# Where the split weights of a hybrid decoder layer begin in SBUF: 48 bytes past a multiple of 64 in place of 0

## What is computed

```python
h = rmsnorm(x, norm1_g)
z = h @ w_in                        # 2048 -> 16400 columns: u, c, b, q, k, v, o, gates, g_a, g_b
a_out = b * causal_conv(c * u)      # 3 taps, with a state of 2 rows for the samples
b_out = sigmoid(o) * mlstm(q, k, v, gates)   # 8 heads, key width 128, value width 256
x = x + (sigmoid(g_a) * a_out + sigmoid(g_b) * b_out) @ w_out      # 2048 x 2048
h2 = rmsnorm(x, norm2_g)
up = causal_conv(h2 @ w_up, state_ffnconv)   # 2048 -> 2 * 5632 columns, 3 taps
x = x + (silu(up[..., 5632:]) * up[..., :5632]) @ w_down           # 5632 x 2048
y = rmsnorm(x, norm_f_g)
```

## Time and profile before

| | us |
|---|---|
| median of 3 runs | 1697.74 |
| profiled execution, its device time | 1698.14 |
| its span, from the first to the last instruction | 1696.4 |
| TensorE matmuls busy | 1684.1 (99%), 13712 matmuls |
| VectorE busy | 1194.5 (70%) |
| ScalarE busy | 767.4 (45%) |
| GpSimd busy | 477.6 (28%) |
| mean granted TensorE clock | 0.998 of 2.4 GHz |

### The profile page before, as it was taken

One profiled execution on the slowest core, in us unless ns is written; L12 is line 12 of the kernel. 1 busy time (PEld: TensorE's weight loads), 2 busy tenths in 40 slices (PEclk: granted clock), 3 DMA queues, 4 the chain that ended last, 5 costly groups with the idle time before them and its releaser, 6 DMA issues.

```text
span 1696.4 us, 37171 instructions
## 1 busy us (share of the span) xinstructions
PE 1684.1 (99%) x13712; PEld 1677.6 (99%) x13712; DVE 1194.5 (70%) x1901; ACT 767.4 (45%) x916; POOL 477.6 (28%) x501
## 2 busy tenths in 40 slices
PE   9999999999999999999999999999999999999997
PEld 8999999999999999999999999999999999999997
DVE  5875857677585766758688877777555777777554
ACT  6545435353443535344445554544333334334443
POOL 4422415242241524224333222222000222222220
PEclk9999999999999999999999999999999999999999
DMA  8788786868878687877766666666666666566663
GB/s 208 189 223 199 199 212 172 212 176 219 192 190 217 166 216 180 212 192 193 195 180 181 190 178 183 180 180 174 183 183 181 180 179 183 174 184 175 186 178 121
DMA packets 591309, 318.80 MB, mean 188 GB/s; under 512 B 17756, under 2 KB 586060, under 8 KB 589156
## 3 DMA queue, kind: packets, MB, share of 16 engines
q1 hardware_dynamic: 578564, 292.99, 64.0%
q10 hardware_dynamic: 10592, 21.57, 5.1%
q0 software_dynamic: 2064, 2.92, 0.8%
HBM read 305.09 MB, written 12.78 MB: 187 GB/s over the span
## 4 chain that ended last, share of the span: by engine, by line
PE 99%; DMA 0%; ACT 0%; DVE 0%; SPq 0%; issue 0%; ACTq 0%; DVEq 0%
PE strip L1526 32%; PE strip L1530 32%; PE strip L1534 32%; PE aux L1408 1%; PE strip L1457 0%; DMA w_raw<-in_w_in 0%; PE aux L1587 0%; PE aux L1477 0%; PE strip L1470 0%; PE aux L1617 0%; PE aux L1616 0%; PE aux L1630 0%; PE aux L1621 0%; PE aux L1614 0%; PE aux L1622 0%; PE aux L1613 0%
## 5 line engine op out<-in xcount | busy, mean ns | idle before, releaser
L714 ACT ACTIVATE w_hi<-w_raw 128x1024 fp32r<-128x1024 f32 x557 | 588.7, 1060 | 786.1 <-PE strip L1534 753.1
L987 DVE TENSOR_TENSOR w_lo<-w_raw,w_hi 128x1024 fp32r<-128x1024 f32 x556 | 710.3, 1282 | 295.0 <-ACT w_hi L714 292.6
L1526 PE MATMUL strip<-xh,w_hi 128*128 128x268 f32 (+1 forms) x2016 | 291.0, 286 | 0.0
L1530 PE MATMUL strip<-xl,w_hi 128*128 128x268 f32 (+1 forms) x2016 | 290.0, 286 | 0.0
L1534 PE MATMUL strip<-xh,w_lo 128*128 128x268 f32 (+1 forms) x2016 | 290.0, 286 | 0.0
L1526 PEld LDWEIGHTS strip<-xh,w_hi 128*128 128x128 f32 x2016 | 265.1, 188 | 0.2
L1530 PEld LDWEIGHTS strip<-xl,w_hi 128*128 128x128 f32 x2016 | 265.2, 188 | 0.0
L1534 PEld LDWEIGHTS strip<-xh,w_lo 128*128 128x128 f32 x2016 | 265.2, 188 | 0.0
L1526 PE MATMUL strip<-x2h,w_hi 128*128 128x266 f32 x1408 | 200.2, 284 | 0.0
L1530 PE MATMUL strip<-x2l,w_hi 128*128 128x266 f32 x1408 | 199.9, 284 | 0.0
L1534 PE MATMUL strip<-x2h,w_lo 128*128 128x266 f32 x1408 | 199.9, 284 | 0.0
(11 more groups left out here) (330 smaller groups left out, 1525.5 us busy)
## 6 DMA issues: line engine op xcount, KB each, us to landing
w_raw<-in_w_in SPq DMA_DIRECT2D x256, 512.0 KB, 4.5
w_raw<-in_w_up SPq DMA_DIRECT2D x176, 512.0 KB, 4.1
w_raw<-in_w_down SPq DMA_DIRECT2D x64, 512.0 KB, 4.1
w_raw<-in_w_out SPq DMA_DIRECT2D x32, 512.0 KB, 4.7
w_raw<-in_w_down SPq DMA_DIRECT2D x32, 384.0 KB, 3.4
out<-c_st ACTq DMA_DIRECT2D x8, 1024.0 KB, 7.1
c_st<-in_state_mlstm_C ACTq DMA_DIRECT2D x7, 1024.0 KB, 10.8
rb<-scratch_rows ACTq DMA_DIRECT2D x8, 270.0 KB, 5.1
```

What stands on the lines that cost most here:

```text
L714: act.activation(w_hi[:, slot, :], w_raw[:, slot, :], ACT.Copy).then_inc(hi_done, 1)
L987: v.tensor_tensor(w_lo[:, slot, :], w_raw[:, slot, :], w_hi[:, slot, :].bitcast(f32), ALU.subtract).then_inc(lo_done, 1)
L1526: pe.matmul(bank[b][:, 0:c1 - c0], w_hi[:, slot, w], rh[:, k0 + k, c0:c1], start=(first and k == 0), stop=False)
L1530: pe.matmul(bank[b][:, 0:c1 - c0], w_hi[:, slot, w], rl[:, k0 + k, c0:c1], start=False, stop=False)
```

## The change

`w_hi` and `w_lo` each get a room of 16896 bytes (512 more than before), begin 32 bytes into it, have slots of 4160 bytes (`WW = 1040` words, 65 x 64 bytes), and leave out the first 4 words of a slot (`WO`). A weight tile so begins at 48 modulo 64 in place of 0. Slots that lay a multiple of 256 bytes apart now lie 4160 bytes apart, which is 64 more than such a multiple. `w_raw` and its DMAs stay as they are. Numbers, kinds, shapes and waits of all instructions are the same; only the addresses change.

`pre_f` is no longer persistent: it lies in the region where the attention has `v_1`, `p_main` and `p_rest`. With 1024 bytes more for the weights and 2816 less for `pre_f` the tensors between them move (`ident`, `ones`, `vecs` by 1024, those after `pre_s` by -1792), and the region by -2048 bytes, which keeps its place modulo 512.

```diff
+    WO = 4
+    WW = KU * P + 16
...
-        w_hi = sb("w_hi", [P, RING, KU * P], f32r)
-        w_lo = sb("w_lo", [P, RING, KU * P], f32r)
+        w_hi_room = (nc.sbuf_base + 31) // 32 * 32
+        sb("w_hi_room", [P, RING * KU * P + P])
+        w_hi = nc.alloc_sbuf_tensor_at("w_hi", [P, RING, WW], f32r, offset=w_hi_room + 32)
+        w_lo_room = (nc.sbuf_base + 31) // 32 * 32
+        sb("w_lo_room", [P, RING * KU * P + P])
+        w_lo = nc.alloc_sbuf_tensor_at("w_lo", [P, RING, WW], f32r, offset=w_lo_room + 32)
...
-        pre_f = sb("pre_f", [P, 2 * FT, NS])
...
+        v_1_0 = cursor[0]
         v_1 = at("v_1", [P, DV])
         p_main = at("p_main", [P, W1], f32r)
         p_rest = at("p_rest", [P, W1], f32r)
...
+        cursor[0] = v_1_0
+        pre_f = at("pre_f", [P, 2 * FT, NS])
...
-                act.activation(w_hi[:, slot, :], w_raw[:, slot, :], ACT.Copy).then_inc(hi_done, 1)
+                act.activation(w_hi[:, slot, WO:WO + KU * P], w_raw[:, slot, :], ACT.Copy).then_inc(hi_done, 1)
...
-                v.tensor_tensor(w_lo[:, slot, :], w_raw[:, slot, :], w_hi[:, slot, :].bitcast(f32),
+                v.tensor_tensor(w_lo[:, slot, WO:WO + KU * P], w_raw[:, slot, :], w_hi[:, slot, WO:WO + KU * P].bitcast(f32),
                                 ALU.subtract).then_inc(lo_done, 1)
...
-                    w = slice(k * P, (k + 1) * P)
+                    w = slice(WO + k * P, WO + (k + 1) * P)
                     pe.matmul(bank[b][:, 0:c1 - c0], w_hi[:, slot, w], rh[:, k0 + k, c0:c1],
                               start=(first and k == 0), stop=False)
```

More of the change, by code:

```diff
@@ L493, in _ @@
             g.wait_ge(first_lo, 1)
-            g.tensor_tensor(w_lo[:, 2, :], w_raw[:, 2, :], w_hi[:, 2, :].bitcast(f32), ALU.subtract)\
+            g.tensor_tensor(w_lo[:, 2, WO:WO + KU * P], w_raw[:, 2, :], w_hi[:, 2, WO:WO + KU * P].bitcast(f32), ALU.subtract)\
              .then_inc(first_lo, 1)
@@ L497, in _ @@
                 g.wait_ge(hi_done, i + 3)
-                g.tensor_tensor(w_lo[:, u, :], w_raw[:, u, :], w_hi[:, u, :].bitcast(f32), ALU.subtract)\
+                g.tensor_tensor(w_lo[:, u, WO:WO + KU * P], w_raw[:, u, :], w_hi[:, u, WO:WO + KU * P].bitcast(f32), ALU.subtract)\
                  .then_inc(lo_done, 2)
@@ L736, in _ @@
                     act.wait_ge(unit_landed[0], 16)
-                    act.activation(w_hi[:, 0, 0:KU * P // 2], w_raw[:, 0, 0:KU * P // 2], ACT.Copy).then_inc(half_hi, 1)
+                    act.activation(w_hi[:, 0, WO:WO + KU * P // 2], w_raw[:, 0, 0:KU * P // 2], ACT.Copy).then_inc(half_hi, 1)
                 if k == 3:
-                    act.activation(w_hi[:, 0, KU * P // 2:], w_raw[:, 0, KU * P // 2:], ACT.Copy).then_inc(hi_done, 1)
+                    act.activation(w_hi[:, 0, WO + KU * P // 2:WO + KU * P], w_raw[:, 0, KU * P // 2:], ACT.Copy).then_inc(hi_done, 1)
                 for kept in (k - 2, k) if k % 4 == 3 else ():
@@ L1036, in _ @@
                     v.wait_ge(hi_done, 1)
-                    v.tensor_tensor(w_lo[:, 0, :], w_raw[:, 0, :], w_hi[:, 0, :].bitcast(f32), ALU.subtract)\
+                    v.tensor_tensor(w_lo[:, 0, WO:WO + KU * P], w_raw[:, 0, :], w_hi[:, 0, WO:WO + KU * P].bitcast(f32), ALU.subtract)\
                      .then_inc(first_lo, 1)
@@ L1043, in _ @@
                         v.wait_ge(hi_done, 3)
-                    v.tensor_scalar(w_hi[:, u, :], w_raw[:, u, :], 1.0, None, ALU.mult).then_inc(hi_done, 1)
+                    v.tensor_scalar(w_hi[:, u, WO:WO + KU * P], w_raw[:, u, :], 1.0, None, ALU.mult).then_inc(hi_done, 1)
             v.wait_ge(lo_done, RING + 4)
@@ L1454, in first_hi @@
                     pe.wait_ge(xl_done, k + 1)
-                    w = slice(k % KU * P, (k % KU + 1) * P)
+                    w = slice(WO + k % KU * P, WO + (k % KU + 1) * P)
                     for t, xt in enumerate((xh, xl)):
@@ L1469, in first_lo_part @@
                     pe.wait_ge(xh_done, k + 1)
-                    mm = pe.matmul(bank[s][:, 0:NT - c0], w_lo[:, 2 * s + h, (k - h * KU) * P:(k - h * KU + 1) * P],
+                    mm = pe.matmul(bank[s][:, 0:NT - c0], w_lo[:, 2 * s + h, WO + (k - h * KU) * P:WO + (k - h * KU + 1) * P],
                                    xh[:, k, c0:NT], start=False, stop=(last and k == KT - 1))
```

## The result

The changed kernel takes 1713.57 us (median of 4 runs, 1712.40 to 1714.83), the kernel before 1698.03 us in the same series (1697.56 to 1701.18). The ratio is 1.0090 (95% interval 1.0078 to 1.0102): it is slower by 0.9%, 15.5 us. The forecast was a gain of 10.6 us, with a range of 1671 to 1709.

What follows compares the result with a forecast made beforehand. TensorE, busy 99%, was taken to bound the kernel by matmul count times step. Weight starts gain 10.6 us, other parts 0: 1697.74 - 10.6 = 1687.1 us; 8-in-10 range 1671 to 1709, the forecast's own 1678 to 1694.

Steps and rivals of the forecast that it cites:

- What bounds the kernel: Whole kernel: TensorE busy 99%, so time is matmuls times a step; only the step or TensorE waits can change it.
- (3): ScalarE's copy and VectorE's difference, writing weights at 48: even 10% longer, nothing reaches TensorE; cost 0.
- (4): `pre_f` on attention buffers: no wait added, 92 us between last read and first write; cost 0.
- (5): Shifts of the remaining buffers and small tensors, which take part in a few dozen matmuls: cost 0.
- Part (1): Weight tile addresses: 13248 weight loads starting at 48 instead of 0 each gain 0.8 ns, 10.6 us in all.
- The pool of 142 us: Matmul steps' excess over one column per cycle, 142 us in all, on which the change can draw.
- The spread of durations: Matmuls of one form last 281 to 288 ns, on `xl` 282 to 297; falling from median to lowest gains 26 us.
- Part (2): Slots 4160 bytes apart: the extra 64 bytes shift the operands' position pattern without changing its mean; 0.
- Rival A: Matmul reads: both operands starting at the same place modulo 64 cost 1.6 ns each; +14.4 us, 1712.1; chance 0.20.
- Rival C: Weight tiles at 48 touch 9 stretches of 64 bytes, not 8: 0.42 ns each, +5.6 us, 1703.3; chance 0.10.
- Rivals B: Weight tile start doesn't matter, the excess is the moving operand's alone: no change, 1697.7; chance 0.20.
- D: Excess from the two reads meeting: a new distance makes the gain several times larger, down to 1671; chance 0.10.

Runs made afterwards that it cites:

- the first experiment: Against the kernel before, only `pre_f` moved onto the attention buffers, with the small tensors' shift, weights as before: 1697.63 us, ratio 1.0002.
- the last one: Against the kernel with only `pre_f` moved: `w_hi` at 48, `w_lo` at 16, tiles 576 bytes apart, slots 64 bytes on, `up_last` on attention buffers: 1716.08 us.
- 48 / 32: Against the kernel with only `pre_f` moved: weights start at 48 modulo 64, six moving-operand buffers go from 48 to 32: 1717.00 us, ratio 1.0119.
- the first map: Against the kernel with only `pre_f` moved: tiles 576 bytes apart, slots 64 bytes on, `w_lo` at 32, `up_last` on attention buffers: 1714.47 us.

## Why the prediction was wrong

*What bounds the kernel* held: step times count, no wait, and all the change is in the step. So did parts (3) and (4), whose costs of nothing the first experiment and the unchanged waits show, and (5), in the same run.

*Part (1) failed, in the sentence "I take the same 0.8 ns for it, as a gain".* The difference between the 280-column strips and the others was read as the price of a start, and the start as a property that weights share. For the moving operand the size was right in the one case tried: 32 in place of 48 costs 0.9 ns at 266 columns with weights at 0. It is the step from there to the weights that fails. The runs show the opposite sign: 0, 16, 32 and 48 for the weights give 121.6, 123.3, 123.3 and 125.0 ns in the first half of the up-projection, and in place of a gain of 10.6 us the start alone costs 20.6. The pool of 142 us gave nothing either: the only form with a lower step in any layout is that of 280 columns in the last one, by 0.3 ns. Held against 13 other layouts, the 121.7 ns at 266 columns is the lowest value of the step that any reaches over the up-projection: three of four constant distances end on it. So with 10.9 ns of excess above the columns, the kernel before stood at the lowest step found in the 4992 matmuls that I hoped to speed up; that nothing lower exists isn't shown. The spread of durations around the medians of 283 and 284, which I took for room below, was misread: at `x2l` it is a cycle around a fixed mean, and the 282 to 297 of `xl` mixes strips of 268 and 280 columns.

*Part (2) failed in "shift that pattern and don't change its mean".* That held at 266 columns with weights at 0 (121.9) and not in the heads: 7.3 us for the slots alone.

*Rival A* gave 1712.1, 1.5 us from the time, for a reason that the runs refute, so that it came so near is luck. It asked for both operands at the same place modulo 64: but weights at 16 or 32 lose 1.7 ns under a moving start of 48, 48 / 32 has 125.0 and 123.3, and the 280-column step rose (128.8 to 129.5) where A has it fall. Rival C, one stretch more, has the right sign for 16, 32 and 48, which all touch 9 stretches; its 0.42 ns is a quarter to an eighth of the 1.7 to 3.4 measured, and it can't give two steps at one set of addresses. Rivals B and D are excluded by the interval. The Trainium skill's 16-byte lines and two independent read ports ("SBUF — State Buffer", "SBUF: two separate sides") would have the weights' start do nothing; here 16 bytes of start cost 1.7 ns, so the measurement decides against that reading.

*What stays open.* Why the step depends on the place. The distance of the two operands doesn't settle it (both moved by 16: slower), nor the weights' start (one distance at 48 reaches 121.8), and the two together don't either. Something is carried over from matmul to matmul: two lasting steps, 123.3 and 125.0, at the same addresses in two runs; and the same constant distance of 176 gave a settled 121.7 in the first map, but 125.5 and 122.6 on `x2h` and `x2l` after other passes on `w_lo`. What it is, and what decides between the two steps, no run here shows. Whether the load of the next weights or the stream of columns is what waits can't be told here, since each matmul has both.

No layout tried is faster than the kernel before.

## What to carry to other kernels

Where TensorE is busy for 99% of the span, 16 to 48 bytes of an operand's start moved the whole kernel by 0.9 to 1.2%: measure the step between starts for each stage, for the layout as a whole, and don't carry a good start from one operand over to the other. Measure it in every stage that runs the same code, too, since two halves with the same addresses can differ by 1.7 ns. Before you look for a gain in the spread of single steps, see whether their mean over a cycle differs anywhere; if all good layouts share it, the kernel may stand at it already.

## What the runs showed of the hardware

With float32r matmuls of 128 x 128 weights and 266 columns, each with its own weight load, the shortest step that lasted over a stage was 121.7 ns in 14 layouts, at the 2.4 GHz level (granted clock 1.00 in the windows), 10.9 ns over one column per cycle. Before, single steps ran from 118 to 125 ns in a fixed cycle of four tiles, alike to within 0.5 ns over 88 units; with weights at 48 one of the four is 132 to 133. The weights' start in 64 bytes was worth up to 3.4 ns of the step (2.8%), and slots 64 bytes further apart 0.4% of the whole time (7.3 us), with TensorE's waits as before. The same addresses ran at 125.0 ns in one half of the up-projection and at 123.3 in the other, in two layouts. ScalarE's and VectorE's writes into the weight buffers left the steps as they were to 0.1 ns at start 48.
